# Convolution projections with rounded split products and the first tap on ScalarE, a rounded mask product, and an end worked by tiles

## What is computed

```python
# attention of the mixer: causal scores (NEG = -1e30 above the diagonal)
# second block: projections of context and sequence, depthwise convolution of 5 taps, silu
pc = hc @ w_in[layer][:, :OFF_CF]
xb_c = silu(dwconv_centred(pc[..., :XB_CH], conv_w[:, :XB_CH], conv_b[:XB_CH]))
p = h @ w_in[layer]
xl = silu(dwconv_centred(p[..., :XB_CH], conv_w[:, :XB_CH], conv_b[:XB_CH]))
cl = silu(dwconv_centred(p[..., OFF_CF:OFF_Z], conv_w[:, XB_CH:], conv_b[XB_CH:]))
...
x = x + g2 * moe_ffn(h2, ...)
return rmsnorm(x, final_norm_w)
```

## Time and profile before

| | us |
|---|---|
| median of three executions | 2759.6 |
| the profiled execution, its own time | 2757.15 |
| its span, first to last instruction | 2755.3 |
| convolution stage with dt, start of L1777 to the first unit | 240.7 |
| busy: PE, DVE, ACT, POOL | 2633.5, 1086.3, 879.5, 56.9 |
| mean granted TensorE clock | 0.970 of 2.4 GHz |

### The profile page before, as it was taken

How to read it: one execution, slowest core, us unless ns; L and a number is a source line. 1 busy time by engine, 2 the same in 40 slices (tenths; PEclk the granted TensorE clock), 3 DMA queues, 4 the chain that set the end, 5 groups by cost and what they waited for, 6 DMA issues and landing times.

```text
span 2755.3 us, 31948 instructions
## 1 busy us (share of the span) xinstructions
PE 2633.5 (96%) x13096; PEld 1754.4 (64%) x13096; DVE 1086.3 (39%) x1695; ACT 879.5 (32%) x1384; POOL 56.9 (2%) x114
## 2 busy tenths in 40 slices
PE   7998979999998889999999999899999999999997
PEld 6887657878876668887888877743443443433433
DVE  4545355555553455556675644511111111111112
ACT  4435325444444244442234454311111111111111
POOL 0000000000000010000010000000000000000000
PEclk9999889999999899999999999999999999999999
DMA  6454454545454454442332233679999999999999
GB/s 247 183 184 172 157 195 168 189 173 198 178 182 174 177 190 183 168 157 94 127 120 92 92 119 135 258 309 425 429 428 429 429 428 428 428 429 428 429 428 414
DMA packets 51739, 700.88 MB, mean 254 GB/s; under 512 B 5874, under 2 KB 6258, under 8 KB 9248
## 3 DMA queue, kind: packets, MB, share of 16 engines
q1 hardware_dynamic: 48640, 688.26, 62.2%
q0 software_dynamic: 3008, 11.33, 1.2%
HBM read 696.43 MB, written 1.05 MB: 253 GB/s over the span
## 4 chain that ended last, share of the span: by engine, by line
PE 91%; DVE 4%; ACT 2%; DMA 1%; issue 1%; POOL 0%; SPq 0%; ACTq 0%; DVEq 0%
PE bank L397 39%; PE bank L2658 24%; PE bank L1712 7%; PE bank L2605 4%; PE bank L2672 2%; PE bank L2648 2%; DVE split_r L374 1%; ACT split_r L365 1%; PE bank L2045 1%; PE bank L2023 1%; DMA ring<-in_stream 1%; PE bank L650 1%; PE bank L920 1%; PE bank L1096 1%; PE bank L1875 1%
## 5 line engine op out<-in xcount | busy, mean ns | idle before, releaser
L397 PE MATMUL bank<-split_r,xT_r 128*128 128x512 f32 (+1 forms) x2880 | 672.7, 395 | 33.7 <-DVE xT_r L568 10.9
L374 DVE TENSOR_TENSOR split_r<-ring,split_r 128x2048 fp32r<-128x2048 f32 (+1 forms) x200 | 455.0, 2276 | 522.5 <-ACT split_r L365 522.1
L397 PEld LDWEIGHTS bank<-split_r,xT_r 128*128 128x128 f32 x2880 | 545.2, 193 | 149.5 <-issue 26.8
L365 ACT CAST split_r<-ring 128x2048 fp32r<-128x2048 f32 (+1 forms) x200 | 378.8, 1896 | 537.2 <-PE bank L397 534.6
L397 PE MATMUL bank<-split_r,work_r 128*128 128x512 f32 x1920 | 462.1, 400 | 0.0
L397 PEld LDWEIGHTS bank<-split_r,work_r 128*128 128x128 f32 x1920 | 360.3, 188 | 93.8 <-issue 7.2
L2658 PE MATMUL bank<-ring,work 128*64 128x512 f32 x1536 | 343.6, 596 | 0.0
L2658 PEld LDWEIGHTS bank<-ring,work 128*64 128x64 f32 x1536 | 107.7, 137 | 229.0 <-issue 229.0
L2658 PE MATMUL bank<-split,work 128*64 128x512 f32 x1024 | 232.2, 595 | 0.0
L1712 PE MATMUL bank<-work,ring 128*128 128x256 f32 x896 | 200.9, 379 | 0.0
L2708 DVE TENSOR_SCALAR work<-bank 128x512 f32<-128x512 f32 x32 | 22.1, 692 | 431.4 <-PE bank L2672 431.4
(11 more groups left out here) (347 smaller groups left out, 2007.5 us busy)
## 6 DMA issues: line engine op xcount, KB each, us to landing
ring<-in_stream SPq DMA_DIRECT2D x224, 2048.0 KB, 9.0
split<-in_stream SPq DMA_DIRECT2D x66, 2048.0 KB, 14.8
work<-in_stream SPq DMA_DIRECT2D x33, 2048.0 KB, 13.4
ring<-in_stream SPq DMA_DIRECT2D x6, 1024.0 KB, 5.7
row<-in_rows POOLq DMA_DIRECT2D x6, 512.0 KB, 4.1
ring<-in_stream SPq DMA_DIRECT2D x2, 1120.0 KB, 6.4
work<-in_conv POOLq DMA_DIRECT2D x2, 768.0 KB, 5.5
x<-in_x SPq DMA_DIRECT2D x1, 1024.0 KB, 5.0
```

The lines of the kernel that those rows point to most:

```text
L365: act.copy(hi, self.part(half)).then_inc(*up("half_hi", half.h))
L374: dve.tensor_tensor(lo, self.part(half), hi.bitcast(F32), ALU.subtract).then_inc(*(self.freed_up(half.chunk.c) if half.ends_chunk else up( ...
L397: mm = self.nc.tensor.matmul(out, a[x][a_at], w[y][w_at], start=start and n == 0, stop=stop and n == 2)
```

## The change

- **Split form for the 56 blocks.** The chunks of the convolution are now split by columns: a half is all the depth and 256 columns, that is two blocks. `pe_conv` makes 24 rounded products per block, of 256 columns each. ACT and DVE split the halves one pair of blocks ahead, at the top of each even turn of their loops. Half 0 is split in the last feed-forward's down projection.
- **The inputs are split too**, the context's in the down projection (`act_context_hi`, `dve_context_lo`), the sequence's at blocks 9 and 10 (`act_x_hi`, `dve_x_lo`) in place of the stage's end. For this `pe_dt(1)` moves from block 24 to block 8, since the plain copy of the sequence is overwritten, and its chunk moves ahead of the x chunks in the stream.
- **First tap on ACT.** The centre tap with the bias is an ACT instruction from the bank (`act_first_tap`). ACT's turn n is: split (n even), first tap n, silu n−1, copy of turn n−2. DVE's is: split (n even), four taps.
- **Mask product.** Identity and mask are rounded once; per unit there are 2 matmuls of 256 columns, ahead of the diagonal scores that add to them.
- **End by tiles.** Last rows, gain, sum, squares, root, scale with the norm's row in one instruction, and the output transfer run for each tile of 128 rows.

```diff
-        for c in (dt_c, bf_c, bb_c, *x_c, dt_c, bf_c, cf_c, bb_c, cb_c, *x_c):
-            w = 2 * NH2 if c == dt_c else 512
-            self.add_chunk(t["stream2"][c, :, 0:KD * w], KD, w, False)
+        for c in (dt_c, bf_c, bb_c, dt_c, *x_c, bf_c, cf_c, bb_c, cb_c, *x_c):
+            if c == dt_c:
+                self.add_chunk(t["stream2"][c, :, 0:KD * 2 * NH2], KD, 2 * NH2, False)
+            else:
+                self.add_chunk(t["stream2"][c], KD, 512, True, True)
...
 # act_ffn, dve_ffn of the last feed-forward
             self.act_context_turned()
-            self.act_split(KF // 2 - 5)
+            self.act_context_hi()
+            self.act_split(KF // 2 - 4)
...
 # pe_scores
-        for pair in range(2):
-            for kb in range(m + 1):
-                c0 = pair * SEQ + kb * P
-                for hh in (2 * pair, 2 * pair + 1):
...
-            for hh in range(2):
-                mm = pe.matmul(bank[2 * (i % 2) + hh][:, c0:c0 + P], self.ident, diag, start=False, stop=True)
+        for kb in range(m + 1):
+            if kb == m:
+                for hh in range(2):
+                    own = bank[2 * (i % 2) + hh][:, :].rearrange("p (a k n) -> p a k n", a=2, k=MT)[:, :, m, :]
+                    pe.matmul(own, self.causal_r[:, 0:P], spread(self.causal_r[:, P:2 * P], 1, 2), start=True, stop=False)
+            for hh in range(4):
...
+    def act_x_hi(self):
+        act.wait_ge(*self.freed_at(self.dt_chunk[0]))
+        act.wait_ge(*at("turn_even", "x1", 5))
+        act.wait_ge(*at("turn_odd", "x1", 7))
+        act.copy(self.hx[0], self.src[1]).then_inc(*up("hx_hi", 0))
+    def dve_x_lo(self):
+        dve.wait_ge(*self.freed_at(self.dt_chunk[1]))
+        dve.wait_ge(*at("hx_hi", 0))
+        dve.tensor_tensor(self.hx[1], self.src[1], self.hx[0].bitcast(F32), ALU.subtract).then_inc(*up("hx_lo", 0))
...
 # pe_conv
+        if n in (0, 24):
+            pe.wait_ge(*at("hx_lo", 0 if n else 1))
+        if n % 2 == 0:
+            self.conv_now = self.pe_take()
...
-            mm = pe.matmul(bank[n % 2][:, 0:SEQ], w[:, k, j * P:(j + 1) * P], self.conv_src(n)[:, k, :],
-                           start=(k == 0), stop=(k == KD - 1))
-        mm.then_inc(*(self.freed_up(ch.c) if j == 3 else up("conv_mm", n)))
+            for i, (a, b) in enumerate(((0, 0), (0, 1), (1, 0))):
+                mm = pe.matmul(bank[n % 2][:, 0:SEQ], w[a][:, k, (n % 2) * P:(n % 2 + 1) * P], h[b][:, k, :],
+                               start=(k == 0 and i == 0), stop=(k == KD - 1 and i == 2))
+        mm.then_inc(*(up("half_used", half.h) if n % 2 else up("conv_mm", n)))
...
+    def act_first_tap(self, n):
+        act.wait_ge(*self.conv_at(n))
+        if n >= 3:
+            act.wait_ge(*(at("conv_turned", n - 3) if self.blocks[n - 3][0] in ("Bc", "Xc", "X")
+                          else at("conv_silu", n - 3)))
+        act.activation(self.acc[n % 3], self.bank[n % 2][:, 0:SEQ], ACT.Identity, scale=wt[:, 2:3],
+                       bias=wt[:, 5:6]).then_inc(*up("tap0", n))
...
 # pe_projections
-            if n == 24:
+            if n == 8:
                 pe.wait_ge(*at("turn_even", "x1", 5))
                 pe.wait_ge(*at("turn_odd", "x1", 7))
                 self.pe_dt(1)
...
 # act_projections
-        for n in range(56):
+        for n in range(58):
             if n in (0, 24):
                 self.act_softplus(n // 24)
-            self.act_conv(n)
+            if n < 56:
+                if n % 2 == 0:
+                    self.act_split(1)
+                self.act_first_tap(n)
+            if 1 <= n <= 56:
+                self.act_conv(n - 1)
+            if n >= 2 and self.conv_turns(n - 2):
+                self.act_conv_turn(n - 2)
...
 # dve_projections
+            if n % 2 == 0:
+                self.dve_split(1)
             self.dve_conv(n)
...
 # pool_out, act_end, dve_end
+        for m in range(MT):
+            pool.wait_ge(*at("final", m))
+            pool.dma_start(t["out"][m * P:(m + 1) * P, :], self.end[:, m, :]).then_inc(*up("dma_out", m))
...
+            dve.scalar_tensor_tensor(self.end[:, m, :], self.x[:, m, :], self.stat[:, 12 + m:13 + m], self.row[:, :],
+                                     ALU.mult, ALU.mult).then_inc(*up("final", m))
```

More of the change, by code:

```diff
@@ L329, in add_chunk @@
             for j in range(n):
-                half = Half(len(self.halves), len(self.halves) % 2, kt // n, width, chunk, j, n)
+                k, w = (kt, width // n) if by_columns else (kt // n, width)
+                half = Half(len(self.halves), len(self.halves) % 2, k, w, chunk, j, n)
                 chunk.halves.append(half)
@@ L699, in act_ffn @@
                 self.act_silu_c()
+                act.wait_ge(*at("rope", 1))
+                act.copy(self.causal_r[:, 0:P], self.ident)
+                act.copy(self.causal_r[:, P:2 * P], self.const("causal")[:, P:2 * P]).then_inc(*up("causal", 0))
             if self.last_ffn and i == 2:
@@ L1756, in dve_conv @@
         acc, src, wt = self.acc[n % 3], self.bank[n % 2], self.conv_w[:, block]
-        dve.wait_ge(*self.conv_at(n))
-        if n >= 3:
-            dve.wait_ge(*(at("conv_turned", n - 3) if self.blocks[n - 3][0] in ("Bc", "Xc", "X")
-                          else at("conv_silu", n - 3)))
-        dve.tensor_scalar(acc, src[:, 0:SEQ], wt[:, 2:3], wt[:, 5:6], ALU.mult, ALU.add).then_inc(*up("tap"))
+        dve.wait_ge(*at("tap0", n))
         for tap in (0, 1, 3, 4):
@@ L1764, in dve_conv @@
             to = acc[:, max(0, -s):SEQ - max(0, s)]
-            dve.wait_ge(*last("tap"))
+            if tap:
+                dve.wait_ge(*last("tap"))
             dve.scalar_tensor_tensor(to, src[:, max(0, s):SEQ - max(0, -s)], wt[:, tap:tap + 1], to, ALU.mult,
@@ new lines, in pe_end, with act_end @@
+                mm = pe.matmul(self.bank[4 + 2 * m + h][:, :], self.PT[rows, m * P:(m + 1) * P], self.yb[rows, :],
+                               start=False, stop=True)
+            mm.then_inc(*up("last_scattered", m))
+    def act_end(self):
+        act, at, up = self.nc.scalar, self.s.at, self.s.up
+        for m in range(MT):
+            for h in range(2):
+                act.wait_ge(*at("x_new", "moe", m, h))
+                if m or h:
+                    act.wait_ge(*self.s.last("sum_sq"))
+                act.activation(self.squares[:, 0:512], self.x[:, m, h * 512:(h + 1) * 512], ACT.Square, scale=D ** -0.5,
+                               accum_out=self.stat[:, 8 + 2 * m + h:9 + 2 * m + h]).then_inc(*up("sum_sq", "end", m, h))
@@ new lines, in dve_end @@
+    def dve_end(self):
+        dve, at, up = self.nc.vector, self.s.at, self.s.up
+        for m in range(MT):
+            dve.wait_ge(*at("last_scattered", m))
+            for h in range(2):
+                cols = slice(h * 512, (h + 1) * 512)
+                dve.tensor_tensor(self.end[:, m, cols], self.bank[4 + 2 * m + h][:, :], self.g2[:, cols],
+                                  ALU.mult).then_inc(*up("out_gained", m, h))
+            for h in range(2):
+                cols = slice(h * 512, (h + 1) * 512)
+                dve.wait_ge(*at("out_gained", m, h))
+                dve.tensor_tensor(self.x[:, m, cols], self.x[:, m, cols], self.end[:, m, cols],
+                                  ALU.add).then_inc(*up("x_new", "moe", m, h))
@@ L2944, in lay_out_2 @@
     for a, b in spans:
-        put(stream[n], ktiles(w, a, b))
+        cuts = (a, a + 256, b) if n in (12, 13, 14, 15, 17, 18, 19, 20) else (a, b)
+        put(stream[n], *(ktiles(w, *ab) for ab in zip(cuts, cuts[1:])))
         n += 1
```

101 lines of the change are left out of this document (48 added, 53 removed).

## The result

The changed kernel takes 2763.4 us in the median of 16 executions, the kernel before 2757.8 in the median of 16: ratio 1.0018, 95% interval 1.0010 to 1.0027. That is 5.7 us more: clear of the noise, within the 8.3 us that I called no change, and 1.4 us from the 2762 on record. Two executions of the kernels further on, one of the mask alone (5352.5 us) and one of the changed kernel without the last loads (2796.1 us), lie far above the others of their kernel and are left out of medians and ratios. The profiled execution of the changed kernel took 2763.61 us. Lines of the changed kernel: L1748 projection pass, L1773 first tap on ACT, L1808 the other taps, L1781 silu, L1796 copy, L370 and L379 split on ACT and DVE, L1917 state, L1935 weighing, L926 mask, L402 split products, L2845 last scatter, L2834 output.

The account below looks back on a forecast made before the run. PE was taken as the bound, moving in the convolution stage to a chain through ACT and DVE. Stage +18, units' start -0.5, mask -10, end -5 gave +2.5 to +3, a 2762 us median; 8-in-10 range 2747 to 2781.

Parts of the forecast that it names:

- idles for over 2 us: PE's clock falls to 1.2 GHz after idling over 2 us; about 10 us of the convolution stage's +18 rest on it.

## What to carry to other kernels

Where a faster engine hands the bound to a loop through two engines that work in written order, look for the one instruction in it that could have run earlier, and ask which event frees its buffer: that place is the earliest, and asking one block sooner, for a buffer still in use, cost 90 us here. A step at the end of a kernel is worth only what the DMA queue leaves of it: add up the bytes still to come behind the last compute step before pricing the steps. A part that gains and one that loses can hide in a kernel that measures nearly the same: here -18.3 and +21.5.

## What I had not expected of the hardware

- Two transfers of 512 KB from POOL's queue landed 2.9 us behind their issue with the DMA engines free, and 8.7 with them filled by 2 MB loads issued before; one of 1 MB took 4.4 and 5.2.
- The eight profiled executions with the new projections and the rounded mask have the same code up to the dt product and reach it up to 5.5 us apart (1179.0 to 1184.5). In the rows a good part of this comes from a weight half that is cast up to a microsecond sooner or later, and from how long the clock stays down behind the wait for it. In both runs with the old projections and the rounded mask the wait in layer 2 is under 2.8 us, with the new ones it is 3.0 to 3.7; why, is open, and no run tried it.
- The length of a wait alone doesn't tell whether the clock falls: behind 2.69 and 2.79 us ahead of two states it stayed at full, behind 2.70 and 2.92 ahead of the other two it was 0.50. In the run without the last loads the same stage has the same waits, 2.79, 2.69, 2.69 and 2.92, and there the second state alone ran at full clock (3.70 us; the others 5.08, 5.24 and 5.40). So the prediction's "idles for over 2 us" holds for the kernel before, where 1.93 us kept the clock and 2.29 did not, but not for the changed one.
